# Three sums kept on chip, and the last norms of a tile group hosted one front part earlier

## The reference

```python
x = x + mixers(rmsnorm(x, norm_mix))                 # gated linear attention + window attention
h = rmsnorm(x, norm_ffn)
# PEER: 8 heads x 16 experts for each token, picked by a product-key top-k
u = take(u_tab, e); act = gelu(einsum('td,thkd->thk', h, u))
v = take(v_tab, e); x = x + einsum('thk,thkd->td', gates * act, v)
gate = sigmoid(rmsnorm(x, norm_ple) @ w_ple_gate)
x = x + gate * (p @ w_ple_proj)
return rmsnorm(x, norm_final)
```

## Time and profile before

| | |
|---|---|
| median of 3 runs | 3534.21 us (3533.68 to 3539.06) |
| the profiled execution's own time | 3534.93 us |
| its span, from the first instruction to the last | 3533.1 us |
| TensorE busy | 80% of the span |
| VectorE busy | 73% |
| ScalarE busy | 40% |
| GpSimd busy | 36% |
| bytes moved by DMA | 1376.57 MB, 390 GB/s over the span |

### The profile page before, as it was taken

The page is one execution under the profiler, slowest core; times in us unless marked ns, Lnnn a source line. Parts: engine busy times, 40 slices in busy tenths (PEclk is TensorE's granted clock), DMA queues, the critical chain, the costliest instruction groups (busy, mean ns, idle before and its releaser), DMA issues.

```text
span 3533.1 us, 35079 instructions
## 1 busy us (share of the span) xinstructions
PE 2829.1 (80%) x11044; PEld 1910.4 (54%) x11044; DVE 2572.2 (73%) x5366; ACT 1409.4 (40%) x3568; POOL 1287.0 (36%) x1028
## 2 busy tenths in 40 slices
PE   8889788987787997777876879978895978657665
PEld 7777566755565865444544637655473635213223
DVE  0247668798878868888777996787768885776664
ACT  2324543434433343444333443444534335334332
POOL 0012233343433244444442443343333433544441
PEclk9999899999998999898987989989998989879887
DMA  6589899999999999999999999999999999999995
GB/s 239 171 313 420 355 416 421 421 401 391 371 405 404 375 390 421 421 416 417 421 421 377 422 409 421 419 419 398 375 406 419 417 390 383 420 421 421 421 422 216
DMA packets 195915, 1376.57 MB, mean 390 GB/s; under 512 B 22401, under 2 KB 24321, under 8 KB 32018
## 3 DMA queue, kind: packets, MB, share of 16 engines
q0 software_dynamic: 147456, 1073.81, 74.0%
q1 hardware_dynamic: 48274, 300.51, 21.4%
HBM read 1363.22 MB, written 11.01 MB: 389 GB/s over the span
## 4 chain that ended last, share of the span: by engine, by line
PE 38%; DMA 28%; DVE 16%; issue 8%; ACT 6%; POOL 2%; DVEq 0%; POOLq 0%; SPq 0%; ACTq 0%
DMA uv<-in_uv,idx 24%; PE bank L597 14%; PE bank L607 10%; PE ysum L789 8%; DVE acc L1331 4%; DVE uv L1303 4%; DMA slab<-in_slabs 3%; POOL uv L554 2%; PE bank L666 2%; DVE lidx L1156 1%; DVE vals L1153 1%; ACT bufX L865 1%; DMA out<-bufA 1%; PE bank L660 1%; DVE bufE L1150 1%
## 5 line engine op out<-in xcount | busy, mean ns | idle before, releaser
L554 POOL DMA_INDIRECT uv<-in_uv,idx x1024 | 1286.8, 1257 | 2189.3 <-PE ysum L789 1004.4
L1303 DVE SCALAR_TENSOR_TENSOR uv<-uv,hbuf 128x1024 f32<-128x1024 f32 x1024 | 1244.8, 1220 | 420.5 <-DMA uv<-in_uv,idx 402.2
L789 PE MATMUL ysum<-uv,diag 128*128 128x512 f32 x2004 | 1059.1, 670 | 417.4 <-ACT diag L1053 412.2
L789 PEld LDWEIGHTS ysum<-uv,diag 128*128 128x128 f32 x2004 | 405.3, 212 | 937.0 <-ACT diag L1053 524.2
L1331 DVE SCALAR_TENSOR_TENSOR acc<-uv,dots,acc 128x1024 f32<-128x1024 f32 x523 | 668.9, 1279 | 107.8 <-ACT dots L1044 91.5
L1039 ACT ACTIVATE dots<-dots 128x2 f32<-128x2 f32 x512 | 102.9, 201 | 1017.2 <-DVE uv L1303 1011.5
L597 PE MATMUL bank<-bufA,slab 128*128 128x256 f32 (+1 forms) x2400 | 440.3, 343 | 14.3 <-DMA slab<-in_slabs 11.0
L597 PEld LDWEIGHTS bank<-bufA,slab 128*128 128x128 f32 x2400 | 391.4, 195 | 84.4 <-issue 32.9
L607 PE MATMUL bank<-slab,bufA 128*128 128x256 f32 x1408 | 317.7, 385 | 7.3 <-DMA slab<-in_slabs 4.7
L607 PEld LDWEIGHTS bank<-slab,bufA 128*128 128x128 f32 x1408 | 270.3, 193 | 61.3 <-issue 17.6
L597 PE MATMUL bank<-bufC,slab 128*128 128x256 f32 (+1 forms) x1280 | 245.0, 353 | 28.7 <-DMA slab<-in_slabs 14.2
(11 more groups left out here) (146 smaller groups left out, 2425.7 us busy)
## 6 DMA issues: line engine op xcount, KB each, us to landing
slab<-in_slabs SPq DMA_DIRECT2D x255, 1024.0 KB
uv<-in_uv,idx POOLq DMA_INDIRECT x1024
x_d<-acc SPq DMA_DIRECT2D x7, 512.0 KB
bufA<-in_x SPq DMA_DIRECT2D x3, 1024.0 KB, 11.8
bufA<-x_d SPq DMA_DIRECT2D x3, 1024.0 KB
out<-bufA SPq DMA_DIRECT2D x3, 1024.0 KB, 12.1
bufE<-in_g_ffn SPq DMA_DIRECT2D x5, 512.0 KB, 9.5
bufX<-in_g_fin SPq DMA_DIRECT2D x5, 512.0 KB
```

Of the source, the lines that this page charges most:

```text
L554: nc.gpsimd.indirect_dma_start(out=uv[:, at % NS, :], out_offset=None, in_=a["uv"], in_offset=bass.IndirectOffsetOnAxis(ap=idx[:, g % 4, k ...
L789: ins = mm(ysum[:, c, :], diag[:, m % DS, :], uv[:, at % NS, D + c * 512:D + c * 512 + 512], start=(m == first), stop=(m == last))
L1303: v.scalar_tensor_tensor(out=row, in0=row, scalar=1.0, in1=hbuf[:, i % HB, :], op0=ALU.mult, op1=ALU.mult, accum_out=dots[:, g % 3, k:k + ...
```

## The change

`acc` gets 3 slots (`AS = 3`), and every tail works on its tiles' slots in `acc`. The array `x2_d` in DRAM goes, with its 7 stores and 4 loads and their semaphores `x2_out` and `x2_in`. A tail's first stage waits for `x2_done`. The result is written by one DMA for each tile instead of one for each group, and a slot is taken again when that write has landed (`tail_out`, now one semaphore for each slot). The ring of diagonals `diag` goes from 3 to 2 slots. `HOST` becomes `{0: 2, 1: 3, 2: 4}`: tail 0 stands in the closing of front part 2, tail 1 in that of 3, tail 2 in that of 4; the closing's order is five `wq` stages, then `T0`, `wq7`, `T1`, `wq8`, then the rest of the tail, 2.5 steps apart, with `T0` not before 3 steps past its group's last tile.

```diff
-DS = 3
+DS = 2
+AS = 3
-HOST = {0: 3, 1: 4}
+HOST = {0: 2, 1: 3, 2: 4}
     if s in GUEST:
         t = [(GUEST[s], n) for n in TAIL]
-        return [t[0], wq[0], t[1], wq[1], t[2], wq[2], t[3], wq[3], t[4], wq[4], t[5], wq[5], t[6], wq[6], t[7], t[8]]
+        return wq[:5] + [t[0], wq[5], t[1], wq[6]] + t[2:]
...
-        pace = 2 if s in GUEST else 1 if s else 0.5
+        pace = 2.5 if s in GUEST else 1 if s else 0.5
         for i, (of, n) in enumerate(closing(s)):
-            stand(of, n, due + math.ceil(pace * (i + 1)))
+            step = due + math.ceil(pace * (i + 1))
+            if n == "T0":
+                step = max(step, PER_TILE * (GROUPS[of][-1] + 1) + 3)
+            stand(of, n, step)
...
-        x2_d = dram("x2_d", (NTILE, P, D))
...
-        acc = sb("acc", [P, 2, D])
-        x2 = [acc[:, (NTILE - 1) % 2:(NTILE - 1) % 2 + 1, :] if q == LAST_GROUP else x1 for q in range(len(GROUPS))]
+        acc = sb("acc", [P, AS, D])
+        x2 = [[acc[:, i % AS, :] for i in tiles] for tiles in GROUPS]
...
                 if at == 0 and n == ("pp" if s == LAST_GROUP else "T0"):
...
                     if s in HOST:
-                        sp.wait_ge(x1_out, 16 * WRITES[HOST[s] + 1])
-                        sp.wait_ge(tile_set, SETS * (HOST[s] + 1))
-                        sp.wait_ge(vec_done, VEC_ORDER[HOST[s], "rt"])
+                        sp.wait_ge(bank_full, USES_END[HOST[s], f"va{last_batch(HOST[s])}"])
                     else:
-                        sp.wait_ge(tail_out, 16 * s)
-                    if s != LAST_GROUP:
-                        for t in tiles_of:
-                            sp.wait_ge(x2_out[t % 2], 16 * (t // 2 + 1))
-                        sp.dma_start(x2[s][:, 0:tt, :], x2_d[t0:t0 + tt].rearrange("t p d -> p t d")).then_inc(x2_in, 16)
-                    if s in HOST:
-                        sp.wait_ge(bank_full, USES_END[HOST[s], f"va{last_batch(HOST[s])}"])
+                        sp.wait_ge(vec_done, VEC_ORDER[s - 1, "T2"])
...
                 if at == 2 and n == "T2":
                     sp.wait_ge(vec_done, VEC_ORDER[s, "T2"])
-                    t0, tt = GROUPS[s][0], len(GROUPS[s])
-                    sp.dma_start(out_t[:, t0:t0 + tt, :], x2[s][:, 0:tt, :]).then_inc(tail_out, 16)
+                    for i in GROUPS[s]:
+                        sp.dma_start(out_t[:, i, :], acc[:, i % AS, :]).then_inc(tail_out[i % AS], 16)
...
                     sp.wait_ge(x1_out, 16 * WRITES[seg_of(i) + 1])
-                    if i >= 2:
-                        sp.wait_ge(x2_out[i % 2], 16 * (i // 2))
-                    sp.dma_start(acc[:, i % 2, :], x1_d[i]).then_inc(acc_in[i % 2], 16)
+                    if i >= AS:
+                        sp.wait_ge(tail_out[i % AS], 16 * (i // AS))
+                    sp.dma_start(acc[:, i % AS, :], x1_d[i]).then_inc(acc_in[i % AS], 16)
...
-                i, at = divmod(n - 3, PER_TILE)
-                if at == 0 and 1 <= i < NTILE:
-                    sp.wait_ge(x2_done, i)
-                    sp.dma_start(x2_d[i - 1], acc[:, (i - 1) % 2, :]).then_inc(x2_out[(i - 1) % 2], 16)
...
-                        if s - 1 in GUEST:
-                            act.wait_ge(tail_out, 16 * (GUEST[s - 1] + 1))
...
-                        if i >= 2:
-                            act.wait_ge(x2_out[i % 2], 16 * (i // 2))
-                        fn(acc[:, i % 2, :], x1[:, 0, :], ACT.Copy).then_inc(tile_set, 1)
+                        if i >= AS:
+                            act.wait_ge(tail_out[i % AS], 16 * (i // AS))
+                        fn(acc[:, i % AS, :], x1[:, 0, :], ACT.Copy).then_inc(tile_set, 1)
...
-                    if s == LAST_GROUP:
-                        act.wait_ge(x2_done, NTILE)
-                    else:
-                        act.wait_ge(x2_in, 16 * (s + 1))
+                    act.wait_ge(x2_done, GROUPS[s][-1] + 1)
...
-                    step(v.tensor_tensor(x2[s][:, 0:tt, :], x2[s][:, 0:tt, :], tp[s][:, 0:tt, :], ALU.add))
+                    for t in range(tt):
+                        step(v.tensor_tensor(x2[s][t], x2[s][t], tp[s][:, t, :], ALU.add))
```

More of the change, by code:

```diff
@@ L395, in build @@
         h_in = [sem(f"h_in{i}") for i in range(HB)]
-        acc_in = [sem(f"acc_in{i}") for i in range(2)]
+        acc_in = [sem(f"acc_in{i}") for i in range(AS)]
         topk_step = sem("topk_step")
@@ L409, in build @@
         ysum_added = sem("ysum_added")
-        x2_out = [sem(f"x2_out{i}") for i in range(2)]
-        x2_in = sem("x2_in")
         tp_in = sem("tp_in")
         gfin_in = sem("gfin_in")
-        tail_out = sem("tail_out")
+        tail_out = [sem(f"tail_out{i}") for i in range(AS)]
         firsts = [(ident[:], a["ident"]), (g_mix[:], a["g_mix"])]
@@ L540, in _ @@
             assert loaded.n == len(LOADS)
-            sp.wait_ge(tail_out, 16 * len(GROUPS))
+            for slot in range(AS):
+                sp.wait_ge(tail_out[slot], 16 * len(range(slot, NTILE, AS)))
         @block.gpsimd
@@ L1000, in stage @@
                 elif n == "T0":
-                    if s == LAST_GROUP:
-                        act.wait_ge(x2_done, NTILE)
-                    else:
-                        act.wait_ge(x2_in, 16 * (s + 1))
-                    square_sums(junk, [(x2[s][:, t, :], stat_t[:, 0, t:t + 1]) for t in range(tt)])
+                    act.wait_ge(x2_done, GROUPS[s][-1] + 1)
+                    square_sums(junk, [(x2[s][t], stat_t[:, 0, t:t + 1]) for t in range(tt)])
                     root(stat_t[:, 1, 0:tt], stat_t[:, 0, 0:tt], D)
@@ L1013, in stage @@
                     for t in range(tt):
-                        fn(tn[:, t, :], x2[s][:, t, :], ACT.Copy, scale=stat_t[:, 2, t:t + 1]).then_inc(tail_scaled, 1)
+                        fn(tn[:, t, :], x2[s][t], ACT.Copy, scale=stat_t[:, 2, t:t + 1]).then_inc(tail_scaled, 1)
                     for f in range(0, KT, 2):
@@ L1024, in stage @@
                     vector_done(act, now, s, "mx")
-                    square_sums(junk, [(x2[s][:, t, :], stat_t[:, 0, TT + t:TT + t + 1]) for t in range(tt)])
+                    square_sums(junk, [(x2[s][t], stat_t[:, 0, TT + t:TT + t + 1]) for t in range(tt)])
                     root(stat_t[:, 1, TT:TT + tt], stat_t[:, 0, TT:TT + tt], D)
@@ L1222, in stage @@
                     for t in range(tt):
-                        step(v.scalar_tensor_tensor(out=x2[s][:, t, :], in0=x2[s][:, t, :],
+                        step(v.scalar_tensor_tensor(out=x2[s][t], in0=x2[s][t],
                                                     scalar=stat_t[:, 2, TT + t:TT + t + 1],
@@ L1324, in add_row @@
                     if i in MOVED:
-                        dve.wait_ge(acc_in[i % 2], 16 * sum(j % 2 == i % 2 for j in MOVED if j <= i))
+                        dve.wait_ge(acc_in[i % AS], 16 * sum(j % AS == i % AS for j in MOVED if j <= i))
                     else:
@@ L1329, in add_row @@
                     dve.wait_ge(ysum_added, 1)
-                row = acc[:, i % 2, :]
+                row = acc[:, i % AS, :]
                 v.scalar_tensor_tensor(out=row, in0=uv[:, at % NS, D:2 * D], scalar=dots[:, g % 3, k:k + 1], in1=row,
@@ L1336, in add_ysum @@
                 dve.wait_ge(v_used_pe, PE_UPTO[last])
-                halves = acc[:, i % 2, :].rearrange("p (c n) -> p c n", c=2)
+                halves = acc[:, i % AS, :].rearrange("p (c n) -> p c n", c=2)
                 v.tensor_tensor(halves, halves, ysum[:], ALU.add).then_inc(done, 1)
```

## The result

The changed kernel takes 3548.01 us (median of 8 runs, 3545.97 to 3551.39) where the kernel before takes 3535.74 us in the runs beside it (8 runs, 3533.03 to 3542.51): a ratio of 1.0031, 95% interval 1.0023 to 1.004. It is 0.3% slower where 0.4% faster was forecast. The profiled execution took 3551.39 us, 3549.6 us of it the span.

The account below looks back on a forecast made before the run. Bound: bytes at DMA's 421 GB/s plateau plus about 263 us lost in dips. Minus 17.4 for bytes, 0 for the plan, plus 2 for diagonals, plus 0.5: minus 15, so 3534 becomes 3519 us; 8-in-10 range 3493 to 3545.

Parts of the forecast that it names:

- What bounds the kernel: Whole kernel: time is all bytes over the 421 GB/s plateau plus about 263 us lost while DMA has too little queued.
- Part 1, the bytes: Stores and loads through DRAM in steps 67 to 453: removing 7.34 MB at 421 GB/s saves 17.4 us in full.
- the bytes were free: Rival: the order of stages bounds, not transfers, so the 17.4 us stay: 3536 us, no change; chance 0.17.
- Part 2, waits: SP's waits at tile ends and tail 2's load wait go; not counted again, being inside their stretches' losses.
- the three stretches that I lowered: Losses in steps 112 to 156, 240 to 284 and 370 to 412: minus 11, minus 4 and minus 4 us.
- Part 3, the fronts: Moved plan, front parts: denser steps 156 to 240 plus 20 us, steps 284 to 370 plus 4 us.
- Part 4, two diagonals: ScalarE waits one row longer with a diagonal: cost between nothing and 53.5 us, taken as 2 us.
- Part 5: Small things: split add in L1217 costs 0.5 us on VectorE; eight result writes and reuse of `acc` slots cost nothing.
- the dense front at 0.49 a step: Rival: steps 156 to 240 and 284 to 370 lose 41 and 42 us, plus 39: 3558 us; chance 0.15.
- the smaller losses: Rival: losses in closings and fronts shrink too and waits weigh 5 us more, minus 24: 3495 us; chance 0.17.
- fronts below 395 GB/s: Sign that the prediction is wrong: the front stretches run below 395 GB/s; about 404 and 405 were expected.

Follow-up runs that it names:

- the pair on the new plan: Kernel before with the changed kernel's hosts, closing order and pace, sums still through DRAM: 3555.11 us; beside it the changed kernel with three diagonals: 3545.55 us.

## Why the prediction was wrong

- **What bounds the kernel**: useful, but not put to the test by the sum, which is true of any kernel. What speaks for it is that mending the dips behind `va` gave 48 us back. What it leaves out is that the two terms depend on each other: bytes that go into a dip cost nothing.
- **Part 1, the bytes, minus 17.4**: the step that failed. "It counts in full, because the stores and loads fall ... inside the stretches that run at 390 to 421 GB/s" is the error in my own words: a stretch at 403 GB/s has room, and a mean doesn't tell whether a transfer falls into a dip. The 6.8 MB put back cost nothing (3546.28 against 3548.01). The rival "the bytes were free" had 0.17, and with the bytes at nothing my own sum would have been 3536.5.
- **The rest of the gap** is sizes. With the bytes put back, so that losses can be compared with those of before, steps 156 to 240 and 284 to 370 lose 28 us more (I took 24), steps 112 to 156, 240 to 284 and 370 to 412 lose 16 us less (I took 19), and steps 412 to 448 their 5 us less, as forecast. Put into my sum these make 3544, and this version takes 3546.28.
- **Part 2, waits**: not counted, and rightly not as far as the traces show; the 9 us of the pair on the new plan have no shown cause. In the changed kernel itself the three stretches that I lowered for the waits and the fewer stages fell by 3.8 and not by 19 us, but 12 us of this gap are the failure of part 1 once more, removed bytes that came back as loss; with the bytes put back they fell by 16.
- **Part 3, the fronts, plus 24**: 25 and 7 us, so 32. Right in sign, sized a little low, and I priced it by the number of stages, which doesn't set the loss by itself: steps 112 to 156 with only the `wq` stages left in them lost 23.8 us, with 19 stages 17.1 or, bytes put back, 14.5. The runs show the cause one level below, the `va` stages with a stage right behind them.
- **Part 4, two diagonals, plus 2**: right within the noise. ScalarE waits 38 us more (I had reckoned 53.5 at most) and the time is the same within 0.1%. The 5 us more of loss in steps 0 to 32 are seen in some profiles with three diagonals too, so they aren't the ring's; their cause is open.
- **Part 5**: a 512 KB result lands in 7.9 us, and nothing waited for it. The rule of the Trainium skill, at least 1 MiB in a DMA ("DMA: Bandwidth & Descriptors", "Rules for kernel authors"), was not put to a test of its own.
- **The rivals**: the dense front at 0.49 a step, 3558, came near in mechanism; the measured losses are 0.33 and 0.30 a step, less than the 0.35 from which I had it decide against the change. What came is a part of this rival together with the free bytes, and I had given chances only to one at a time. In the smaller losses a term is off by one: from 8 to 2 us is minus 6, not 7. Of the signs, fronts below 395 GB/s didn't come (400 and 402), so this one was set too low to warn.

Partly open: why spacing all of the attention brings so much less than spacing `va` alone. The first leaves one empty step behind each `va` of parts 3 and 4 and none behind three of the four in part 2, the second leaves two nearly everywhere. But in part 3 the first also shows a new dip at steps 236 and 237 (`wo3`, `rt`; 290 GB/s over 18 us) that the second has not (416), though the stages there stand at almost the same steps.

## What to carry to other kernels

Before a removed transfer is counted, look whether DMA has room where it stands: bytes in a dip are free, and they seem to begin to cost when the dips are mended. Where time is split into bytes over a rate and a rest, the rest can grow by all that the bytes give up. Price a denser plan by its worst stage and not by its mean. A stage in which two in-order engines wait for each other in turn holds every other queue; here the ten gather slots covered one such hold and not a second wait right behind it, so such a stage wants empty steps behind it. A change can be sound and still lose, because it takes these steps away; the same change was 12 us slower on one spacing and 22 us faster on another (with three diagonals).

## What the runs showed of the hardware

The DMA engines held 421 GB/s over 190 us (changed kernel, steps 412 to 448) and over 268 us (kernel before, steps 448 to 496), with gathers, slab loads and stores in the queues together. The 18 us at 248 GB/s behind `va1` lost as much as 3 MB take at 421. TensorE was busy 17.31 us of these 18 at a granted clock of 0.99: here a TensorE at full load was no sign that the transfers were fed.
